# A four-layer block in float32: down projections as three float32r products, their remainders on VectorE, and two norms with one round of sums

## What is computed

```python
# first block, layers first0 and first1
h = rms_norm(x, norm_ffn_g[layer]) * (1.0 + scale_f) + shift_f
y = swiglu(h, w1, w3, w2)        # first0: (silu(h @ w1) * (h @ w3)) @ w2, D_FF = 2816
y = moe_swiglu(...)              # first1: 8 experts, top 2
x = x + gate_f * y
...
x = rms_norm(x, final_norm_g)    # behind first1
# second block, layers even and odd
hm = rms_norm_2(x, norm_mix[i]) * (1.0 + sc_m) + sh_m
...
gate = causal_dwconv(gate, conv_w) + conv_b      # 3 taps
x = x + g_f * ((silu(gate) * val) @ w_down)      # D_FF = 2816
```

## Time and profile before

| | |
|---|---|
| median of three runs | 2569.79 us (2569.15 to 2570.77) |
| the profiled execution | 2563.78 us, its span 2562.0 us |
| PE busy | 2496.2 us, 97% |
| PE weight loads busy | 2170.4 us, 85% |
| DVE busy | 1773.8 us, 69% |
| ACT busy | 1199.0 us, 47% |
| POOL busy | 333.2 us, 13% |
| HBM read | 653.76 MB, 256 GB/s over the span |
| first up product of the dense feed forwards | `first0` 194.56 us, `even` 1824.02 us, `odd` 2351.58 us |

### The profile page before, as it was taken

The page is one execution under the profiler, slowest core; times in us unless marked ns, Lnnn a source line. Parts: engine busy times, 40 slices in busy tenths (PEclk is TensorE's granted clock), DMA queues, the critical chain, the costliest instruction groups (busy, mean ns, idle before and its releaser), DMA issues.

```text
span 2562.0 us, 36960 instructions
## 1 busy us (share of the span) xinstructions
PE 2496.2 (97%) x14304; PEld 2170.4 (85%) x14304; DVE 1773.8 (69%) x1949; ACT 1199.0 (47%) x1273; POOL 333.2 (13%) x97
## 2 busy tenths in 40 slices
PE   5999999999999999999999999898999999999999
PEld 4889998878888888888888888788999899998998
DVE  5832775768888888888888888455379788873112
ACT  3213213117667676767676767322312356663221
POOL 0005550000000000000000000001344200002552
PEclk8999999999999999999999999999999999999999
DMA  8745884766989898989898989330478543442442
GB/s 365 316 164 206 347 318 183 301 246 252 363 321 363 322 362 318 363 320 362 321 363 318 362 321 362 124 136 17 160 306 316 227 165 135 146 148 99 166 175 86
DMA packets 90383, 656.18 MB, mean 256 GB/s; under 512 B 10032, under 2 KB 10288, under 8 KB 10800
## 3 DMA queue, kind: packets, MB, share of 16 engines
q1 hardware_dynamic: 80928, 589.34, 60.9%
q10 hardware_dynamic: 9360, 65.52, 6.4%
HBM read 653.76 MB, written 1.05 MB: 256 GB/s over the span
## 4 chain that ended last, share of the span: by engine, by line
PE 72%; issue 17%; POOL 6%; DVE 3%; ACT 1%; ACTq 0%; DMA 0%; POOLq 0%; DVEq 0%; SPq 0%
PE bank L1164 71%; POOL ring_rounded L737 6%; PE bank L1709 1%; DVE work L1862 1%; DVE rstd L1910 0%; DVE xT L1856 0%; DMA ring<-stream_dram 0%; DVE ring L1862 0%; PE bank L1533 0%; DVE ring_rounded L1850 0%; DVE yT L1856 0%; ACTq L758 0%; ACT work_rounded L778 0%; POOL work L697 0%; PE bank L1635 0%
## 5 line engine op out<-in xcount | busy, mean ns | idle before, releaser
L1850 DVE TENSOR_TENSOR ring_rounded<-ring,work_rounded 128x2048 fp32r<-128x2048 f32 x372 | 842.3, 2290 | 159.4 <-ACT work_rounded L912 122.1
L1164 PE MATMUL bank<-work_rounded,proj_rounded 128*128 128x512 f32 x1792 | 614.3, 406 | 0.6 <-DVE proj_rounded L1850 0.2
L912 ACT ACTIVATE work_rounded<-ring 128x2048 fp32r<-128x2048 f32 x224 | 428.5, 1914 | 0.0
L1164 PEld LDWEIGHTS bank<-work_rounded,proj_rounded 128*128 128x128 f32 x1792 | 338.0, 189 | 76.9 <-issue 2.9
L1164 PE MATMUL bank<-ring_rounded,proj_rounded 128*128 128x512 f32 x896 | 353.6, 395 | 0.0
L1164 PE MATMUL bank<-work_rounded,ff_hid_rounded 128*128 128x512 f32 x896 | 302.3, 398 | 1.8 <-DVE ff_hid_rounded L1850 1.8
L1164 PE MATMUL bank<-yT_rounded,ring_rounded 128*128 128x256 f32 x960 | 271.6, 283 | 0.0
L1164 PE MATMUL bank<-hT,ring 128*128 128x256 f32 x1088 | 243.3, 384 | 1.1 <-ACT hT L802 1.1
L1164 PEld LDWEIGHTS bank<-hT,ring 128*128 128x128 f32 x1088 | 208.1, 192 | 36.4 <-issue 8.6
L1164 PE MATMUL bank<-ff_hid,ring 128*128 128x256 f32 x1056 | 232.9, 379 | 0.0
L1164 PEld LDWEIGHTS bank<-ff_hid,ring 128*128 128x128 f32 x1056 | 198.4, 190 | 25.9
(11 more groups left out here) (286 smaller groups left out, 4299.5 us busy)
## 6 DMA issues: line engine op xcount, KB each, us to landing
ring<-stream_dram SPq DMA_DIRECT2D x561, 1024.0 KB, 4.8
work<-stream_dram ACTq DMA_DIRECT2D x56, 1024.0 KB, 9.1
params<-params_dram ACTq DMA_DIRECT2D x1, 1728.5 KB, 28.6
consts<-consts_dram ACTq DMA_DIRECT2D x1, 1568.0 KB, 37.5
cond<-cond_dram ACTq DMA_DIRECT2D x2, 512.0 KB, 3.8
xT<-x_dram ACTq DMA_DIRECT2D x1, 1024.0 KB, 10.4
out_dram<-xT SPq DMA_DIRECT2D x1, 1024.0 KB, 3.9
consts<-consts_dram ACTq DMA_DIRECT2D x1, 577.0 KB, 32.0
```

The lines of the kernel that those rows point to most:

```text
L912: act.activation(up_high[u][half], ring[:, (moe_first + s + half) % RING, :], ACT.Copy)\
L1164: return pe.matmul(o, lhsT=a, rhs=b, start=start, stop=stop, skip_group_check=True)
L1850: return dve.tensor_tensor(o, a, b, op)
```

## The change

Four things, all in place in one kernel:

1. Down blocks 0 to 9 of each dense feed forward are made by `mm3` as well: 48 float32r products instead of 16 in float32. down(10) stays as it was. For it ScalarE makes a third high part per chunk (into two new buffers in `work`) and the high part of the hidden values (`ff_hid_high`, 128 x 512, in the place of `h_heads`), and their low part is made by VectorE (`hidden_low`).
2. All remainders of weights, three per chunk now, are VectorE's (`weights_low`). GpSimd is left with the low part of `h`, once a layer. Line L1850 of before is L1902 now, L1853 L1905, L1856 L1908 and L1862 L1914.
3. ScalarE makes the first high part of a chunk ahead of `load_modulation`, and VectorE makes one block of modulation between the second and third remainder and two behind the third.
4. The norm of `x` behind the experts and the first norm of `even` share a round of sums. With r the first factor and g the first gain, the second mean of squares is r squared times the sum of g squared times x squared, so both sums are made of `xT` at once (in banks 4 and 5), and `yT` of `even` comes from `xT` with both factors (`gain_both`, `twice_mean`) before `xT` itself is scaled. GpSimd's first work of `first1` waits for `weights_used` and `split_low` too.

```diff
+SPLIT_DOWN = ("first0", "even", "odd")
+LOWS_ON_DVE = ("first0", "even", "odd")
...
+        ff_down_high = [work_r[:, mod_at + (MOD_GROUP + u) * SLOT:mod_at + (MOD_GROUP + 1 + u) * SLOT] for u in range(2)]
+        ff_hid_high, ff_hid_low = (rounded["h_heads"][:, a * 4 * T:(a + 1) * 4 * T].rearrange("p (b t) -> p b t", b=4)
+                                   for a in range(2))
...
+        split_buffers = [w_high[0], w_high[1], ff_down_high[0], w_high[2], w_high[3], ff_down_high[1]]
+        down_split = [kind in SPLIT_DOWN for kind in plan]
+        split_width = [3 if split else 2 for split in down_split]
...
+                    pool.wait_ge(weights_used, place[f"in{n}"])
+                    pool.wait_ge(split_low, splits_before[n])
...
+                if plan[n] not in LOWS_ON_DVE:
...
+                if follows_final(u):
+                    act.wait_ge(*final_vec.at("mean", 0))
+                    act.activation(twice_mean, twice_mean, ACT.Sqrt, bias=EPS, scale=1.0 / D)\
+                       .then_inc(norm_act.sem, KD + 1)
...
+                    if not final:
+                        high(c, odd, 0)
                     if n + 1 < len(plan) and not isinstance(c, int):
                         load_modulation(n + 1, c - 2)
-                    if not final:
-                        high(c, odd, 0)
...
                     if not (isinstance(c, int) and c == 0) and not final:
                         high(c, odd, 1)
+                    if down_split[n] and not final:
+                        act.wait_ge(ffn_hid, base + 2 * c + 2)
+                        if not isinstance(c, int) or c >= 2:
+                            act.wait_ge(weights_used, c * 3 + (first - 1))
+                        act.activation(ff_hid_high[:, 2 * odd:2 * odd + 2, :], ff_hid[:, 2 * odd:2 * odd + 2, :], ACT.Copy)\
+                           .then_inc(hid_high, 1)
+                        high(c, odd, 2)
...
+                if follows_final(u):
+                    return
...
+                if which == 2:
+                    for k in range(KD):
+                        pe.wait_ge(*norm_vec.at(f"s{k}", u))
+                        last = mm(bank(5, 0, T), const("ones"), yT[:, k, :], k == 0, k == KD - 1)
+                    last.then_inc(*norm_pe.step("sum"))
...
+                    plain = final or not down_split[n]
...
+                            if plain:
+                                last = mm(o, down_k(at)[:, j, d * P:d * P + P], ff_hid[:, b, :], start, final and j == 1)
+                            else:
+                                last = mm3(o, [p[:, j, d * P:d * P + P] for p in parts],
+                                           (ff_hid_high[:, b, :], ff_hid_low[:, b, :]), start, False)
...
+            def final_norm(u):
...
+                for k in range(KD):
+                    stt(yT[:, k, :], xT[:, k, :], gain_sq[:, k:k + 1], xT[:, k, :], ALU.mult, ALU.mult)\
+                        .then_inc(*norm_vec.step(f"s{k}"))
+                root_inverse(u)
...
+                tt(twice_mean, bank(5, 0, T), rstd[:, :], ALU.mult).then_inc(*final_vec.step("scaled"))
...
+                tt(twice_mean, twice_mean, rstd[:, :], ALU.mult).then_inc(*final_vec.step("mean"))
+            def norm_of_normed(n, u):
...
+                tt(gain_both, gain_next, gain[:, :], ALU.mult).then_inc(*norm_vec.step("gain"))
...
+                dve.reciprocal(twice_mean, twice_mean).then_inc(*norm_rstd.step("rstd"))
...
+                for k in range(KD):
+                    stt(yT[:, k, :], xT[:, k, :], gain_both[:, k:k + 1], twice_mean, ALU.mult, ALU.mult)\
+                        .then_inc(*norm_vec.step(f"s{k}"))
...
+                for k in range(KD):
+                    last = stt(xT[:, k, :], xT[:, k, :], gain[:, k:k + 1], rstd[:, :], ALU.mult, ALU.mult)
...
+                    weights_low(0)
                     for j in range(2):
...
                         tt(ff_hid[:, b, :], bank(4 + b, T, 2 * T), ff_silu[:, b, :], ALU.mult).then_inc(ffn_hid, 1)
-                    if n + 1 < len(plan) and not isinstance(c, int):
-                        mod_parts(n + 1, c - 2, range(MOD_GROUP))
+                    weights_low(1)
+                    modulate(range(1))
+                    hidden_low()
+                    if down_split[n]:
+                        weights_low(2)
+                    modulate(range(1, MOD_GROUP))
```

More of the change, by code:

```diff
@@ L385, in build_program @@
         norm_rstd = steps("norm_rstd", "rstd")
+        final_vec = steps("final_vec", "sq scaled mean gain root x")
+        twice_mean, gain_sq, gain_next, gain_both = (
+            ff_mid[:, 0, :], *(ff_mid[:, 1, a * KD:(a + 1) * KD] for a in range(3)))
         norm_vec = steps("norm_vec", "gain " + " ".join(f"s{k}" for k in range(KD)))
@@ L554, in build_program, with follows_final @@
             norms += [(n, 0), (n, 1)] + ([(n, 2)] if kind == "first1" else [])
+        def follows_final(u):
+            return u > 0 and norms[u - 1][1] == 2
         def x_ready(u, k=KD - 1):
@@ L727, in feed_forward @@
             def feed_forward(n):
-                first, before = place[f"ffn{n}"] + 2, dense_before[n] * SPLITS
+                first, before, width = place[f"ffn{n}"] + 2, splits_before[n], split_width[n]
                 pool.wait_ge(*high_act.at("h", dense_before[n]))
@@ L783, in norm @@
                     act.wait_ge(x_here, 16)
-                for k in range(KD):
+                for k in range(0 if follows_final(u) else KD):
                     if u:
@@ L1100, in high @@
                         act.wait_ge(weights_used, c * 3 + (first + w - 3))
[L1101 removed]
+                    act.activation(split_buffers[3 * odd + w], ring[:, (first + at) % RING, :], ACT.Copy)\
                        .then_inc(split_high, 1)
@@ L1216, in norm @@
                 else:
-                    keep_running(14 if plan[n] == "odd" and which == 0 else 7)
+                    keep_running(14 if plan[n] == "odd" and which == 0 else 7, 0 if which == 2 else 5)
             def normed(n, which, k):
@@ L1925, in norm @@
             def norm(n, which):
                 u = norms.index((n, which))
+                if which == 2:
+                    return final_norm(u)
+                if follows_final(u):
+                    return norm_of_normed(n, u)
                 if which == 0:
@@ L1944, in norm @@
                 for k in range(KD):
-                    o = xT if which == 2 else yT
-                    stt(o[:, k, :], xT[:, k, :], gain[:, k:k + 1], rstd[:, :], ALU.mult, ALU.mult)\
+                    stt(yT[:, k, :], xT[:, k, :], gain[:, k:k + 1], rstd[:, :], ALU.mult, ALU.mult)\
                         .then_inc(*norm_vec.step(f"s{k}"))
```

115 lines of the change are left out of this document (81 added, 34 removed).

## The result

The changed kernel takes 2539.8 us (median of 4 runs, 2539.4 to 2544.0) where the kernel before takes 2569.5 (4 runs, 2565.5 to 2570.8). The ratio is 0.9891, its 95% interval 0.9878 to 0.9904: 29.7 us less. Forecast were 2547.0 us, 22.8 less than the kernel before, with a range from 2536 to 2558. So the sign and the places are right, and 7 us of gain were left out.

A forecast was written before the change was run, and what follows sets the result against it. TensorE was taken as the bound (71% of the chain). Gains of 13.8 us in `first0`, 2.7 in `even`, 4.6 in `odd` and 1.7 in norms, 22.8 together, gave 2541.0, plus 6.0 to the median: 2547.0 us, range 2536 to 2558.

The forecast's parts named there:

- clock behind the stop: After each stop in `even` and `odd`, TensorE runs 3.4 us at half rate, losing 1.7 us.
- Down blocks: 48 products at 0.12 us take 5.76 us, a chunk 17.28: 11.4 us gained per layer, 34.2 in all.
- VectorE's chunk in `even`: In chunks 2 to 9, VectorE's 18.3 us of work exceeds TensorE's 17.28 and becomes the bound, costing 6.8 us.
- Rival A: Everything hides: no stop at chunk 0, no VectorE excess; gain 43.1 us, time 2526.7; chance 0.04.
- The stop ahead of up(1): At chunk 0 TensorE waits 5.1 us for convolution and remainder, once in `even`, once in `odd`; `first0` escapes.
- `odd`'s margin of 0.4 us: Mid-loop in `odd`, the first remainder is over at 2456.0, TensorE asks at 2456.45; it fits by 0.4 us.
- rival B: Handovers add 1 us per chunk, 7 us in `even` and 5.4 in `odd`: 2559.4 us; chance 0.12.
- ScalarE: nothing: One more high part and copy of 512 columns per chunk on ScalarE, busy 47% of the span, cost nothing.
- The norms: Merged sums behind the experts let `yT` start 1.7 us earlier; bounds a loss of 1.6 and a gain of 4.
- The rule that was weighed: HBM loads bound at about 358 GB/s per core would make `first0` chunks 17.57 us, the forecast 2549.3.
- rival C: DMA at 350 GB/s makes a chunk of `first0` 17.97 us, 5.5 us lost: 2552.5 us; chance 0.08.
- rival D: Late modulation groups in `load_modulation` lengthen chunks of `first0` and `even`: 2566 to 2588 us; chance 0.06.

The follow-up runs named there:

- Run 9: run 8 with ScalarE's first tap of the convolution in `even` moved ahead of the modulation's loads; 2521.9 us, ratio 0.9822.
- run 6: Changed kernel, but in chunk 0 of `even` and `odd` VectorE makes the first two remainders ahead of the convolution; 2525.8 us, ratio 0.9828.
- Run 7: Changed kernel with 44 products of ones by ones on TensorE ahead of up(1) in `even` and `odd`; 2545.3 us, ratio 0.9904.
- run 1: Changed kernel with dense down slots in float32 and remainders on GpSimd again; merged norms and ScalarE's new order stay; 2581.8 us, ratio 1.0046.
- run 5: run 1 with ScalarE issuing the modulation's loads ahead of a chunk's first high part again; 2569.2 us, ratio 0.9998.
- run 12: Changed kernel with the modulation's loads issued ahead of the chunk's first high part again; 2550.0 us, ratio 0.9930.
- run 11: Changed kernel with all three remainders of a chunk on GpSimd, down slots still split; 2635.3 us, ratio 1.0259.
- run 8: run 6 plus ScalarE making the convolution's first tap in `even`, behind the modulation's loads; 2541.3 us, ratio 0.9892.
- first0_alone: Changed kernel with split down slots and VectorE's remainders in `first0` alone, merged norms kept; 2561.2 us, ratio 0.9965.

## Why the prediction was right, and where its terms were off

| Term | forecast | profile of the change |
|---|---|---|
| chunk that TensorE bounds | 17.28 us | 17.18 |
| `first0` | 13.8 | 14.7 |
| `even`: VectorE's excess | 6.8 | 158.05 - 154.62 = 3.4 |
| `even` and `odd`: stop | 5.1 each | 5.0 each |
| clock behind the stop | 1.7 each | 1.6 and 2.5 |
| `even` in all | 2.7 | 13.8 - 5.0 - 1.6 = 7.2 |
| `odd` in all | 4.6 | 12.4 - 5.0 - 2.5 = 4.9 |
| norms | 1.7 | 1.1 |
| sum | 22.8 | 27.9, medians 29.7 |

- *Down blocks.* Right in kind. The price of 0.12 us is that of the up block and holds there (11.50 us for 96); in the down block 48 products take 5.68 us, 0.118 each, where the sum had 5.76. With the 0.02 of the up block that is 0.10 us per chunk and 3.1 over 30, less than half of what was missing. The split of the old chunk was misread: 11.52 left out the 0.18 us at the start of an up block, and they were counted to the down block (6.90 for 6.72). As only the sum of the two entered, this cost nothing.
- *VectorE's chunk in `even`.* The mechanism is right, the size is the step that failed: 18.3 us were added up from lengths that overlap, and, for 0.08 of it, from the convolution of a VectorE that waits for the second bank. Rival A names the 0.08 us by which the pieces overlap, and the sum didn't use them. At 17.70 the term is 3.4. Run 9 shows that it was VectorE's.
- *The stop ahead of up(1)* and that `first0` escapes it: right, and by run 6 the whole price of two stops with their clock is 14 us for an order that nothing needed. Run 7 shows that TensorE's standing still takes the clock down.
- *`odd`'s margin of 0.4 us.* It held in all nine chunks (154.62 us); rival B has no gap to show. Rival A falls with the two stops and VectorE's 17.70 us.
- *ScalarE: nothing.* The sum was right, the reason was incomplete. The prediction took the new order of ScalarE as given and did not see that its arithmetic for `first0` depends on it. Runs 1, 5 and 12 show what it is worth.
- *GpSimd* off the chain: right, and run 11 shows why the third remainder could not go there. GpSimd's remainders and VectorE's operations on SBUF wait for each other for whole instructions. In run 1 the dot product that starts at 1944.04 ends at 1949.61, 1.10 us after GpSimd's remainder beside it, which ends at 1948.51; the next remainder takes 5.56 us where one alone takes 4.60. So a dot product of 1.22 us lasts up to 5.6 us and a low part of 0.69 up to 5.1, while a convolution out of banks keeps its 1.89 us. The Trainium skill, "SBUF — State Buffer", section "Who interferes with whom", says just this: a VectorE operation with two inputs in SBUF and a GpSimd operation that reads SBUF exclude each other until the one is through. The rows agree with it.
- *The norms.* 2.1 us sooner in the profile, 1.0 given back in the next products; run 5 can't tell them from nothing. That nearly the forecast size came out is not shown to be more than luck.
- *The clock in stretches the change does not touch.* The sum had no term for it. It is chance by runs 6 to 8, and most of the reason why the two profiled executions are 19.8 us apart where the terms come to 27.9 and the medians to 29.7. A forecast could lie several us off by it alone.
- *DMA.* In three chunks of `even` in run 9 the core reads 366 GB/s for 51.5 us while TensorE has no gap, and the chunks of `first0` take 17.18 us. The rule that was weighed, about 358 GB/s from HBM, would have made them 17.57; it does not bind here. The Trainium skill's "HBM Reference", section "Specifications (TRN2)", calls that figure the share of a core whose neighbour reads too, which this kernel on one core has not. Rivals C and D fall with it.

Open stays why `first0` gained 3 us more against run 1 than the rows of its loop give. In the records of the five executions each, the granted clock is 0.9844 on average in run 1 and 0.9858 in first0_alone; as shares of the span at half rate these are 40 and 36 us lost, an estimate that covers the 3 us. No run shows why the two differ, nor what decides how long the clock is low in `first1`.

## What to carry to other kernels

Add up an engine's period from start to start in a stretch where that engine is late, not from lengths and not from a stretch in which it waits: 0.6 us of 18 were the difference between 6.8 and 3.4 us lost. When work moves to an engine, look at the first iteration too, where the order written for the steady loop stands behind something that isn't needed yet; there, moving two operations forward gave half as much as the whole change. And when a step waits for one engine (here the issue of loads on ScalarE, which waits for VectorE's dot products), ask what stands behind it in the same program and who needs that, and when. The same swap, the high part ahead of the loads, gained 10 us where VectorE makes the remainders and waited for it, and cost 12.6 where it let GpSimd start its remainders beside VectorE's dot products.

## What was not expected of the hardware

- A low part of 128 x 512 on VectorE took 5.09 us beside a GpSimd remainder, 7 times its 0.69: it waited out the rest of the other engine's instructions first.
- Float32 products of 128 x 128 ones by 128 columns leave two records each, and 44 of them took 9.99 us, 0.227 each; float32r products of 256 columns are 0.118 us apart in the down blocks and 0.120 in the up blocks.
- An up block whose products follow a float32 down block took 11.70 us, and 11.50 behind a float32r one, though nothing in it had changed.
- Two stops of the same length (5.12 us from product to product) cost 1.6 us of clock in one layer and 2.5 in the other; the stretch at half clock was over by 1838.9 in the one and 2361.1 in the other, 3.4 and 5.4 us after TensorE went on.
